# Attention of an encoder step on one core: values as stationary high and low parts, turned probabilities of two heads moving, and another order of rounding and exponentials for wide rows

## What is computed

```python
# selection of keys is done earlier: scores holds 0 for a selected key, a large negative number for others
s = jnp.einsum('btngd,btknd->btngk', q, k_sel) * (HEAD_DIM_A ** -0.5)
s = jnp.where(sel_ok[:, :, None, None, :], s, -jnp.inf)
p = jax.nn.softmax(s, axis=-1)
o = jnp.einsum('btngk,btknd->btngd', p, v_sel)
```

## Time and profile before

| | us |
|---|---|
| median of 3 runs (2986.15 to 2987.56) | 2987.25 |
| the profiled execution | 2985.07 |
| its span | 2983.1 |
| `attend`, first to last work in the trace | about 1483 to 1678 |
| of it the 64 prompt units | about 1490 to 1649 |

### The profile page before, as it was taken

The page is one execution under the profiler, slowest core; times in us unless marked ns, Lnnn a source line. Parts: engine busy times, 40 slices in busy tenths (PEclk is TensorE's granted clock), DMA queues, the critical chain, the costliest instruction groups (busy, mean ns, idle before and its releaser), DMA issues. The chain is left out here.

```text
span 2983.1 us, 43644 instructions
## 1 busy us (share of the span) xinstructions
PE 2848.5 (95%) x15997; PEld 2668.6 (89%) x15997; DVE 1646.6 (55%) x2944; ACT 847.9 (28%) x1474; POOL 377.8 (13%) x499
## 2 busy tenths in 40 slices
PE   8999999999999999999889789799899999999998
PEld 8999999999989799999878578688799999999997
DVE  5444444444451378899354367577644444444445
ACT  4111111111132334554276335311321111111112
POOL 0000000000010044444230266300000000000000
PEclk9999999999999999999989799899999999999999
DMA  4111111111022122222210323432121111111111
GB/s 149 43 42 42 42 42 42 42 42 42 8 56 45 29 62 82 83 90 90 76 40 10 86 63 81 145 126 68 43 64 43 42 42 42 42 42 42 42 35 64
DMA packets 234890, 172.47 MB, mean 58 GB/s; under 512 B 45481, under 2 KB 216217, under 8 KB 234786
## 3 DMA queue, kind: packets, MB, share of 16 engines
q1 hardware_dynamic: 227634, 142.70, 16.8%
q10 hardware_dynamic: 4752, 18.94, 1.7%
q0 software_dynamic: 2400, 9.44, 0.8%
HBM read 136.51 MB, written 34.47 MB: 57 GB/s over the span
## 5 line engine op out<-in xcount | busy, mean ns | idle before, releaser
L523 DVE TENSOR_TENSOR ffn_prod<-ffn_silu,ffn_p_up 128x384 f32<-128x384 f32 x132 | 73.1, 554 | 759.2 <-ACT ffn_silu L431 759.2
L506 DVE SCALAR_TENSOR_TENSOR x<-ffn_p_down,x 128x512 f32<-128x512 f32 x738 | 474.9, 685 | 1.3 <-PE ffn_p_down L156 1.3
L156 PE MATMUL ffn_p_gate<-ffn_hT_hi,ffn_g_hi 128*128 128x384 f32 x1056 | 355.8, 337 | 6.2 <-issue 3.8
L156 PE MATMUL ffn_p_gate<-ffn_hT_lo,ffn_g_hi 128*128 128x384 f32 x1056 | 354.2, 335 | 0.0
L156 PE MATMUL ffn_p_gate<-ffn_hT_hi,ffn_g_lo 128*128 128x384 f32 x1056 | 354.2, 335 | 0.0
L156 PE MATMUL ffn_p_up<-ffn_hT_hi,ffn_u_hi 128*128 128x384 f32 x1056 | 353.6, 335 | 0.0
L156 PE MATMUL ffn_p_up<-ffn_hT_hi,ffn_u_lo 128*128 128x384 f32 x1056 | 353.0, 334 | 0.0
L156 PE MATMUL ffn_p_up<-ffn_hT_lo,ffn_u_hi 128*128 128x384 f32 x1056 | 352.8, 334 | 0.0
L431 ACT ACTIVATE ffn_silu<-ffn_p_gate 128x384 f32<-128x384 f32 x132 | 64.9, 492 | 860.9 <-PE ffn_p_up L156 860.9
L156 PE MATMUL ffn_p_down<-o_c_hi,o_t_lo 128*128 128x512 f32 x756 | 295.3, 391 | 0.0
L156 PE MATMUL ffn_p_down<-o_c_lo,o_t_hi 128*128 128x512 f32 x756 | 294.8, 390 | 0.0
(11 more groups left out here) (388 smaller groups left out, 5109.6 us busy)
## 6 DMA issues: line engine op xcount, KB each, us to landing
ffn_raw_g<-in_ffn_w_gate SPq DMA_DIRECT2D x44, 512.0 KB, 4.9
ffn_raw_u<-in_ffn_w_up SPq DMA_DIRECT2D x44, 512.0 KB, 6.1
ffn_raw_d<-in_ffn_w_down SPq DMA_DIRECT2D x44, 512.0 KB, 3.7
h_raw<-in_w_in SPq DMA_DIRECT2D x32, 512.0 KB, 3.9
projected_d<-sp_stage ACTq DMA_DIRECT2D x20, 576.0 KB, 2.8
conv_d<-sp_stage ACTq DMA_DIRECT2D x12, 576.0 KB, 3.3
dl_qkv<-conv_d SPq DMA_DIRECT2D x27, 256.0 KB, 4.1
x<-in_x_prompt SPq DMA_DIRECT2D x8, 512.0 KB, 7.1
```

Of the source, the lines that this page charges most:

```text
L156: mm = nc.tensor.matmul(out, stationary(k)[a], moving(k)[b], start=(start and at == 0 and i == 0), stop=(stop and 3 * at + i == n - 1))
L506: nc.vector.scalar_tensor_tensor(out=xs, in0=p_down[(NO * q + o) % 4][:], scalar=0.5, in1=xs, op0=ALU.mult, op1=ALU.add).then_inc(added, 1)
L523: nc.vector.tensor_tensor(prod[:, slot], silu[:, slot], p_up[slot][:, 0:TG], ALU.mult).then_inc(prod_done, 1)
```

## The change

In prompt units the values are made stationary. `v_parts` holds them as a high part (columns 0 to 63) beside the rest (64 to 127); the turned probabilities are kept as `turned_hi` (ACT, rounded to float32r) and `turned_lo` (DVE, the difference), two units of a pair side by side, and both move past the values, 256 columns each. The output thus comes out turned: rows 0 to 63 of `p_o` for the high part of the values, 64 to 127 for the rest, a group of 4 heads (one t and kv) in 512 columns. ACT's `keep_low` copies the lower half, DVE's `join` adds the upper one, and multiplies by the reciprocal sums, which PE's `spread_totals` lays over 64 rows from diagonal blocks (`put_on_diagonal`). `turn_out`, `keep_out` and the prompt's `norm` go. The units of a tile are ordered by kv first. `masked` goes; the masked scores are written to `prob` and the exponential works in place. `split` makes three copies in place of two for each kv. For rows of more than 512 keys ACT does `keep_turned(u)` ahead of `exp(u+1)`, for others behind it as before.

```diff
-        units = [(t, j, kv) for t in range(NTP) for j in range(4) for kv in range(KV)] + [
+        units = [(t, j, kv) for t in range(NTP) for kv in range(KV) for j in range(4)] + [
...
+            return [g for g in range(LAST_GROUP + 1) if u == (DEC + 1 if g == LAST_GROUP else 4 * g + 6)]
...
@@ @block.tensor
                 else:
                     pe.wait_ge(tail_kept, i)
+                    pe.wait_ge(scaled, 1)
...
+            def weigh(pair, half=None):
+                g, first = pair // 2, pair % 2 == 0
+                tile, kv = g // KV, g % KV
+                n = tile + 1
+                out = p_o[:, pair % 2 * 2 * P:(pair % 2 + 1) * 2 * P]
+                for k in range(n) if half is None else range(n * half // 2, n * (half + 1) // 2):
+                    if k == 0:
+                        pe.wait_ge(turned_rest, before[2 * pair + 2])
+                        pe.wait_ge(v_low, KV)
+                        if g and first:
+                            pe.wait_ge(joined, g)
+                    nc.tensor.matmul(out, v_parts[:, kv, k, :], turned_hi[:, pair % 2, k].rearrange("p h q -> p (h q)"),
+                                     start=(k == 0 and first), stop=False)
+                    mm = nc.tensor.matmul(out, v_parts[:, kv, k, :], turned_lo[:, pair % 2, k].rearrange("p h q -> p (h q)"),
+                                          start=False, stop=(k == n - 1 and not first))
...
+            def spread_totals(g):
+                pe.wait_ge(diag_ready, 4 * g + 4)
+                if g:
+                    pe.wait_ge(scaled, g)
+                pe.wait_ge(tail_kept, 3 if g else 1)
+                nc.tensor.matmul(p_oT[0:HD].rearrange("p h q -> p (h q)"), const.rest[:, ONES, 0:HD], diag[:, g % 2, :],
+                                 start=True, stop=True).then_inc(spread_over, 1)
...
                 turn(u)
-                if u >= 1:
-                    weigh(u - 1)
+                for g in joined_at(u):
+                    spread_totals(g)
+                if 2 <= u < DEC:
+                    weigh(u // 2 - 1, u % 2)
+                if u == DEC:
+                    weigh(2 * LAST_GROUP + 1)
+                if u > DEC:
+                    weigh_dec(u - 1)
...
@@ @block.vector
-                if max(same_place(u), u - 3) > 0:
-                    dve.wait_ge(exped, max(same_place(u), u - 3))
+                if u >= 4:
+                    dve.wait_ge(exped, u - 3)
                 if t < NTP:
-                    nc.vector.tensor_tensor_reduce(masked[:, at:at + width], p_s[:, at:at + width],
+                    if same_place(u):
+                        dve.wait_ge(prob_turned, before[same_place(u)])
+                    nc.vector.tensor_tensor_reduce(prob[:, at:at + width], p_s[:, at:at + width],
...
+            def put_on_diagonal(u):
+                g, j = u // 4, u % 4
+                if g >= 2 and j == 0:
+                    dve.wait_ge(spread_over, g - 1)
+                nc.vector.tensor_scalar(diag[:, g % 2, j * P:(j + 1) * P], const.ident[:], rtotal[:, j:j + 1], None,
+                                        ALU.mult).then_inc(diag_ready, 1)
+            def keep_rest(u):
+                pair = u // 2
+                for i in range(groups[u]):
+                    dve.wait_ge(turned_high, before[u] + i + 1)
+                    ks = slice(4 * i, min(4 * i + 4, cols(u)[1] // P))
+                    nc.vector.tensor_tensor(turned_lo[:, pair % 2, ks, u % 2, :], p_pT[(before[u] + i) % 2][:, 0:ks.stop - ks.start, :],
+                                            turned_hi[:, pair % 2, ks, u % 2, :].bitcast(F32), ALU.subtract).then_inc(turned_rest, 1)
...
+            def join(g):
+                dve.wait_ge(low_kept, g + 1)
+                nc.vector.tensor_tensor(out_sum[:], p_o[0:HD, :], out_sum[:], ALU.add).then_inc(joined, 1)
+                dve.wait_ge(joined, g + 1)
+                dve.wait_ge(spread_over, g + 1)
+                if g >= 2:
+                    dve.wait_ge(stored[g % 2], 16 * (g // 2))
+                nc.vector.tensor_tensor(oT[:, g % 2], out_sum[:].rearrange("p (h q) -> p h q", h=4), p_oT[0:HD],
+                                        ALU.mult).then_inc(scaled, 1)
...
-                if u >= 1:
-                    norm(u - 1)
+                for g in joined_at(u):
+                    join(g)
+                if u < DEC:
+                    if u == 0:
+                        for kv in range(KV):
+                            split_values(kv)
+                    keep_rest(u)
+                invert(u)
+                if u < DEC:
+                    put_on_diagonal(u)
+                if u > DEC:
+                    norm_dec(u - 1)
...
@@ @block.scalar
                     nc.scalar.copy(swapped[other[kv], kv, mine], qkT[own[kv], 4, mine])
-                    nc.scalar.copy(parts[own[kv], kv, :, mine], qkT[own[kv], :, mine]).then_inc(split_hi, 1)
+                    nc.scalar.copy(keys[own[kv], kv, mine], qkT[own[kv], 4, mine])
+                    nc.scalar.copy(queries[own[kv], kv, t % 3], qkT[own[kv], 0:4, mine]).then_inc(split_hi, 1)
...
+            def keep_low(g):
+                act.wait_ge(weighed, 2 * g + 2)
+                if g:
+                    act.wait_ge(scaled, g)
+                nc.scalar.copy(out_sum[:], p_o[HD:P, :]).then_inc(low_kept, 1)
...
-                if u + 1 < U:
+                for g in joined_at(u):
+                    keep_low(g)
+                wide = cols(u)[1] > 512
+                if u + 1 < U and not wide:
                     exp(u + 1)
-                keep_turned(u)
+                if u < DEC:
+                    if u == 0:
+                        for kv in range(KV):
+                            keep_values(kv)
+                    keep_turned(u)
+                else:
+                    keep_turned_dec(u)
+                if u + 1 < U and wide:
+                    exp(u + 1)
```

More of the change, by code:

```diff
@@ L1490, in _ @@
                     turn_tail(u - BATCH_S // 2 - 1)
-                if u % HEADS == 2 and HEADS < u <= DEC + 2:
-                    turn_out(u // HEADS - 1)
                 if u >= DEC + 3:
                     turn_out_dec(u - DEC - 3)
-            weigh(U - 1)
+            weigh_dec(U - 1)
             for b in range(BATCH_S - 3, BATCH_S):
@@ new lines, in norm_dec @@
+            def norm_dec(u):
+                j = units[u][1]
+                q = slice(u % 4, u % 4 + 1)
+                dve.wait_ge(weighed, 2 * LAST_GROUP + 3 + u - DEC)
+                if j >= 2:
+                    dve.wait_ge(o_turned, j - 1)
+                for half in own:
+                    mul = nc.vector.tensor_scalar(o_dec[half, j % 2, :], p_o[half, half], rtotal[half, q], None,
+                                                  ALU.mult)
+                mul.then_inc(normed, 1)
@@ L1570, in exp @@
                     act.wait_ge(inverted, u - 3)
-                src = masked if units[u][0] < NTP else p_s
+                src = prob if units[u][0] < NTP else p_s
                 nc.scalar.activation(prob[:, at:at + width], src[:, at:at + width], ACT.Exp, bias=shift[:, q],
@@ L1593, in keep_out @@
-            def keep_out(t):
-                act.wait_ge(o_turned, t + 1)
-                if t >= 2:
-                    act.wait_ge(stored[t % 2], 16 * (t // 2))
-                nc.scalar.copy(oT[:, t % 2], p_oT[:]).then_inc(oT_ready, 1)
+                pair = u // 2
+                if pair >= 2:
+                    act.wait_ge(weighed, pair - 1)
+                for i in range(groups[u]):
+                    act.wait_ge(prob_turned, before[u] + i + 1)
+                    ks = slice(4 * i, min(4 * i + 4, cols(u)[1] // P))
+                    nc.scalar.copy(turned_hi[:, pair % 2, ks, u % 2, :],
+                                   p_pT[(before[u] + i) % 2][:, 0:ks.stop - ks.start, :]).then_inc(turned_high, 1)
@@ new lines, in keep_turned_dec @@
+            def keep_turned_dec(u):
+                at, width = cols(u)
+                if u == DEC:
+                    act.wait_ge(tail_stored, 96)
+                if u >= DEC + 2:
+                    act.wait_ge(weighed, 2 * LAST_GROUP + 2 + u - DEC - 1)
+                act.wait_ge(prob_turned, before[u] + 1)
+                bank, full = p_pT[before[u] % 2], width // P
+                nc.scalar.copy(probT[:, u % 2, 0:full * P].rearrange("p (k q) -> p k q", k=full), bank[:, 0:full, :])
+                nc.scalar.copy(probT[0:SEQ_S, u % 2, full * P:(full + 1) * P], bank[0:SEQ_S, full, :]).then_inc(
+                    probT_ready, 1)
@@ L1599, in keep_out_dec, with keep_values @@
+            def keep_values(kv):
+                nc.scalar.copy(v_parts[:, kv, :, 0:HD], va[:, 0:NTP, own[kv]]).then_inc(v_high, 1)
+            def keep_low(g):
[3 more added lines that the diff above has]
+                nc.scalar.copy(out_sum[:], p_o[HD:P, :]).then_inc(low_kept, 1)
             def keep_out_dec(i):
-                act.wait_ge(o_turned, NTP + 4 * i + 4)
```

(1 more changed line is left out.)

144 lines of the change are left out of this document (63 added, 81 removed).

## The result

The changed kernel took 2996.99 us (median of 5, 2994.26 to 2998.19), the kernel before beside it 2986.15 (2984.36 to 2987.56): ratio 1.0038, 95% interval 1.0025 to 1.0051. That is 10.8 us slower, where 7 were forecast; the median forecast was 2994, and the range 2978 to 3003 holds what came. The span of the profiled execution, the shortest of the five, went from 2983.1 to 2992.5 us.

What follows compares the result with a forecast made beforehand. PE was taken as the bound with wide rows, DVE becoming it after the change. DVE's 145.4 us plus start, splits, loop and blocks gave 168.7 for the prompt units; with first split and sequences, +7.1: 2994, range 2978 to 3003.

Steps and rivals of the forecast that it cites:

- The sum: All terms for the 64 prompt units: 168.7 us against 159.3 before; whole kernel +7.1 with first split and sequences.
- DVE with narrow rows: Tiles 0 to 3: DVE's work sets the pace, 0.99, 1.27, 1.53 and 1.79 us a unit without join.
- DVE with wide rows: Tiles 4 to 7: DVE's sum is the bound, 2.13 to 2.93 us a unit without join, ACT's loop within 0.2.
- Join: DVE's add and product over 512 columns, 15 times in the prompt units, 1.31 us each.
- Splits: DVE runs dry behind ACT's split: 2.15 us each at u = 8, 16, 24, 1.8 each at 32 and 40.
- Start: Tile 0: late copies and waits for stores make it 18.7 us, 9.2 above DVE's work; 1.5 more in tile 1.
- Diagonal blocks: On DVE, two or three blocks behind each split meet POOL's work: 1 us in all, between 0 and 6.
- Sequences: After the prompt units: less PE lag and the last turn_out gone, 2.5 us less in all.
- Rival 1: PE's clock falls to half behind the splits, costing 6 to 10 us: 3002; chance 0.15.
- Its signs: In the prompt units: DVE 75 us busier, full in tiles 2 and 3, ahead of PE in tile 7; clock 1.00 from tile 2.
- The loss with narrow rows: Rival: ACT and DVE run further ahead and hide split and start costs, 5 to 8 us less: 2987; chance 0.17.
- the wide gain: Rival: in tiles 4 to 7 DVE is not the bound and PE's full 17 us come in: about 2977; chance 0.14.

Runs made afterwards that it cites:

- a2: Changed kernel with the diagonal blocks written by POOL in place of DVE; ratio 1.0024 to the kernel before, prompt units 168.4 us against 173.8 in the changed kernel.
- e1: Changed kernel without the rests of the turned probabilities and with each group's first pair weighed whole behind the next unit's turning; ratio 0.9999, prompt units 162.7 us.
- d1: Changed kernel with each group's first pair weighed whole behind the next unit's turning, not in halves; ratio 1.0034 to the kernel before, prompt units 172.5 us.
- a3: Changed kernel without the rests of the turned probabilities (one element handled, high part weighed twice); ratio 1.0021 to the kernel before, prompt units 169.1 us.
- b2: Changed kernel with three places for the convolution's last rows, so ACT's copies wait for no store; ratio 1.0039 to the kernel before, prompt units 170.0 us.
- b1: Changed kernel with eight idle matmuls on PE in the gap behind each of five splits; ratio 1.0035 to the kernel before, prompt units 172.1 us.

## Why the prediction was right, point by point

- **The sum: in part luck.** Its own prices, laid out by tile, give about 72 us for tiles 0 to 3 and 96.6 for tiles 4 to 7; measured are 72.2 and 101.6. So the 5.1 us by which the prompt units missed (168.7 forecast, 173.8 measured) lie with wide rows, and the gain of about 2 there became a loss of 2.1. Half of the miss was made up by 1.8 us at the end of the stage and behind it, for which it had no term, and by 0.8 at the stage's start (0.25 later forecast, 0.5 earlier measured); without these the time would have been 2.6 us further off. With narrow rows errors of both signs cancel: tiles 0 and 1 were put too high, tiles 2 and 3 too low. (In the term for the start, tile 0 by DVE's prices is 8 times 0.99 and a join, 9.2 and not 9.5.)
- **DVE with narrow rows: right.** `keep_rest` stands at 0.60 from start to start for 512 columns, alone 0.68, the prices read from the earlier trace rows; DVE's busy time in the eight stretches is 148.7 us, the sum was 145.4. Ordinary units of tile 3 take 1.79 to 1.85 (1.79 forecast), and a2, and e1 beside d1, show that DVE's work is what counts there.
- **DVE with wide rows: the number was right, the engine wasn't.** DVE's sum and ACT's loop were both put at 2.93 in tile 7, and the sum went by DVE. It is ACT's loop: 2.37, 2.58, 2.80 and 3.01 measured, 2.31, 2.52, 2.73 and 2.93 forecast. Most of the 0.07 is the time from the end of the row's sum to the first copy, 0.80 (1646.93 to 1647.73) in a3, where 0.74 had been added up. Over some 26 units that is 1.8 us.
- **Join: right in size, and the warning beside it too.** The step's masking was put at 5.6 us behind `exp(58)` and the scores at 5.5; measured from 1642.63 they are 5.68 and 5.42. The cost was 1.31, and is 0.9 to 1.2 in tiles 6 and 7. That either path alone would keep it there was not said, though the two numbers said it.
- **Splits: right mechanism, somewhat too large.** 10.1 against 7.5 given back by eight small copies, which keep some cost. DVE's waits behind the five splits are 1.5 to 1.8 us each, where 2.15 and 1.8 had been put.
- **Start: 18.7 forecast, 17.8 measured**; the wait for the stores is there (below), and b2 takes 2.3 us of tile 0 and 1.2 of tile 1 away.

```profile
1506.90 0.57 ACT L1725 COPY at_probT<-at_p_oT 27x512 f32<-27x512 f32 x1 [3.63 <-DMA out_new_conv_s<-at_probT]
```

- **Diagonal blocks: 1 us taken, between 0 and 6.** 7 of 64 are slow (0.49 to 1.16, others 0.28 or 0.29), 4.5 us of DVE beyond their price; how much of it lay on the path was not told apart. Each of the seven ends 0.09 us behind an instruction of POOL that overlaps it, as the first pair shows:

```profile
1493.83 0.95 POOL L1383 MEMSET at_spread<- 128x1024 f32 x1
...
1493.77 1.10 DVE L1575 TENSOR_SCALAR at_diag<-ident,at_rtotal 128x128 f32<-128x128 f32 x1
```

  By the rule cited in the prediction (the Trainium skill, "SBUF — State Buffer", "Who interferes with whom") a tensor_scalar in a two-port mode that issues second waits until POOL's instruction ends. The trace agrees on the end in all seven, and on the order in six; in the pair shown the block was the first by 0.06 us by the recorded starts, which is within what spans on POOL are good for. The subtraction, with one input in PSUM, took 0.28 at 1493.38 beside POOL, its price alone.
- **Sequences: -2.5 forecast, -2.8 measured, but not at the place forecast.** From the first to the last exponential of them 15.9 us go by in place of 18.6. The forecast counted from `exp(63)` to the end of the first sequence's weighing, 10.7 before and 9.1 to come; measured it is 10.8 (1659.45 to 1670.26), because the last join's step (3.95, before 2.09) lies in it. That step belongs to the prompt units as well, so the two terms of the sum overlap by it.
- **PE: 0.11 a weighing forecast, 0.12 measured; `spread_totals` 0.86, measured 1.07, and 1.14 to the next start.**
- **What was missing, 5 us of the 14.5.** Three terms are of that size; of them b1 tried the clock, the other two are read from the trace alone. Rival 1 was taken as another outcome; it came beside the forecast, at 1.7 us by b1. ACT's loop, 1.8. And the passage from two units ahead to one, between tiles 3 and 4, had no term: a join and the first wide masking fall together there. DVE works without a pause from 1556.70 to 1561.79, ACT waits 2.78 us for a shift, and PE waits 0.54 for a bank that the subtraction frees, the wait that I had costed at nothing because the next use is a whole unit away. Unit 32 is the first that fills two banks, and the second of them holds unit 31, whose copy and subtraction come only behind `exp(32)`:

```profile
1561.83 0.83 ACT L1658 ACTIVATE at_prob<-at_prob,at_shift 128x640 f32<-128x640 f32 x1 [2.78 <-DVE at_shift L1563]
...
1564.00 0.33 PE L1461 MATMUL at_p_pT<-ident,at_prob 128*128 128x128 f32 x1 [0.54 <-DVE at_turned_lo L1583]
```

  The steps 31 and 32 take 4.2 and 3.5 us there, before 3.7 and 2.0: 2 us. The start gives 0.9 back.
- **Its signs.** DVE is busy 69.2 us more in the stage (75 forecast); tiles 1 to 3 take 54.4 us and tile 7 26.8, neither in what would have made it wrong. Three signs failed: DVE was to be full in tiles 2 and 3 and is busy for 84% and 89% of them; in tile 7 it was to be ahead of PE, and PE is busy 26.01 us, DVE 25.42; the clock was to be 1.00 from tile 2 on and was 0.90 and 0.93 in tiles 2 and 4.
- **The other rivals.** The loss with narrow rows was not hidden; the wide gain came as 0.6 us in tile 7 and 1.6 in tile 6 only, and tiles 4 and 5 lost more than that; the weighing was not held to 0.19.

## What to carry to other kernels

When work moves from a full engine to an idle one, add up the new engine's whole step for each width of row: the gain hoped for here (PE's, with wide rows) and the loss (DVE's, with narrow ones) belong to different tiles, and the gain ended where the next engine's loop began. When two paths through a step come out within 0.1 us of each other, write both down as bounds, because removing either alone can show nothing. A long copy in one piece on an engine whose neighbour is only one or two units ahead costs most of its length (waits of 1.5 to 1.8 us for 2.3 here); cut into pieces, one to a unit, most of that came back.

## What the runs showed of the hardware

- After a gap of some 2 us in tile 4 PE had the lower clock for most of 4 us (0.62 and 0.53), and idle matmuls in the gap kept the upper one; the two tiles where this was so were 0.8 us shorter each (b1). In tile 5 nearly the same gap left the clock at 1.00 in one kernel and not in another (d1: 0.64 and 0.51, the tile 0.6 us longer).
- POOL writes a 128 by 128 diagonal block in 0.60 us, DVE in 0.28. It pays all the same where DVE sets the pace (5.5 us in tiles 1 to 3).
- A diagonal block on DVE that meets an instruction of POOL ends 0.09 us behind that instruction: 0.49 to 1.16 us in place of 0.28, seven times of 64. Four that met only its last 0.06 to 0.12 us kept 0.29.
